# A linear recurrence in eight chunks: one copy changes engine, and the finishing of each chunk's outputs moves from a stage of its own into the next chunk

## The reference, cut to what matters

```python
def step(state, inp):                       # for each of 1024 tokens, per head
    r_t, w_t, k_t, v_t, kk_t, a_t = inp
    sa = jnp.einsum('bhvk,bhk->bhv', state, -kk_t)
    state = (state * w_t[:, :, None, :] + sa[..., None] * (kk_t * a_t)[:, :, None, :]
             + v_t[..., None] * k_t[:, :, None, :])
    return state, jnp.einsum('bhvk,bhk->bhv', state, r_t)
...
mu = jnp.mean(y, axis=-1, keepdims=True)    # group norm over the 64 values of a head
var = jnp.mean(jnp.square(y - mu), axis=-1, keepdims=True)
y = ((y - mu) * lax.rsqrt(var + RWKV_GN_EPS)).reshape(B, S, C)
y = y * lnx_g.astype(f32) + lnx_b.astype(f32)
bonus = jnp.sum((r_h * k_h * r_k).astype(f32), axis=-1, keepdims=True) * v_h.astype(f32)
y = (y + bonus.reshape(B, S, C)) * g.astype(f32)
```

## Time and profile before

| | us |
|---|---|
| three runs | 3178.64, 3179.79, 3193.91 |
| median | 3179.79 |
| profiled execution, its own time | 3191.28 |
| its span, first to last instruction | 3189.7 |
| `rwkv_chunks`, 601 to 973 | 372 |
| `rwkv_outputs`, 973 to 1018.8 | 46 |
| engines busy over the span | PE 2767.5, DVE 1088.9, ACT 632.5, POOL 514.5 |

### The profile page before, as it was taken

How to read it: one execution, slowest core, us unless ns; L and a number is a source line. 1 busy time by engine, 2 the same in 40 slices (tenths; PEclk the granted TensorE clock), 3 DMA queues, 4 the chain that set the end, 5 groups by cost and what they waited for, 6 DMA issues and landing times. The chain is left out here.

```text
span 3189.7 us, 52841 instructions
## 1 busy us (share of the span) xinstructions
PE 2767.5 (87%) x19900; PEld 2592.0 (81%) x19901; DVE 1088.9 (34%) x2428; ACT 632.5 (20%) x1210; POOL 514.5 (16%) x753
## 2 busy tenths in 40 slices
PE   8899897588883979893999999999999999999980
PEld 7876685377773968793999999999999999999980
DVE  2118322344545322434322222232232232322228
ACT  3119412112213122320111011111111111111111
POOL 0000001333330000015112121211212212112104
PEclk9999998799996989896999999999999999999995
DMA  7110111000002120216888778888888888887877
GB/s 236 31 33 1 40 46 28 9 17 18 18 11 73 40 73 14 62 41 197 292 287 292 256 262 281 288 295 287 295 282 293 294 287 282 294 283 262 283 240 270
DMA packets 340492, 549.48 MB, mean 172 GB/s; under 512 B 41120, under 2 KB 120864, under 8 KB 340384
## 3 DMA queue, kind: packets, MB, share of 16 engines
q1 hardware_dynamic: 321056, 505.56, 46.4%
q0 software_dynamic: 19360, 42.87, 4.6%
HBM read 507.06 MB, written 41.31 MB: 172 GB/s over the span
## 5 line engine op out<-in xcount | busy, mean ns | idle before, releaser
L2385 PE MATMUL experts_up<-experts_xs,g_pieces 128*128 128x144 f32 (+1 forms) x8192 | 1035.7, 289 | 66.6 <-issue 38.0
L2385 PEld LDWEIGHTS experts_up<-experts_xs,g_pieces 128*128 128x128 f32 x8192 | 1029.1, 197 | 73.7 <-issue 73.7
L2408 PE MATMUL experts_down<-experts_hs,g_across 128*128 128x144 f32 (+1 forms) x3072 | 394.6, 289 | 3.8 <-issue 3.3
L2408 PEld LDWEIGHTS experts_down<-experts_hs,g_across 128*128 128x128 f32 x3072 | 387.6, 190 | 7.7 <-issue 7.6
L2267 POOL DMA_INDIRECT experts_x<-h_rows,experts_index x198 | 191.7, 968 | 1146.9 <-DVE experts_xs L2314 1092.1
L2344 DVE TENSOR_SCALAR experts_glu<-experts_up,experts_bias 128x176 f32<-128x176 f32 x256 | 102.5, 400 | 712.5 <-PE experts_up L2385 712.5
L2294 ACT ACTIVATE experts_sig<-experts_glu 128x352 f32<-128x352 f32 x128 | 63.6, 497 | 963.4 <-DVE experts_lin L2346 963.4
L2301 ACT ACTIVATE experts_yT<-experts_down,experts_bias 128x176 f32<-128x176 f32 x256 | 99.7, 406 | 394.8 <-PE experts_down L2408 142.7
L2335 DVE COPY experts_bias<-g_bias 128x24 f32 x32 | 5.8, 180 | 400.8 <-ACT experts_yT L2301 400.8
L2397 PE MATMUL experts_down<-experts_hs,g_across 128*128 128x144 f32 (+1 forms) x1024 | 133.2, 288 | 0.0
L2397 PEld LDWEIGHTS experts_down<-experts_hs,g_across 128*128 128x128 f32 x1024 | 130.1, 190 | 0.0
(11 more groups left out here) (414 smaller groups left out, 4097.5 us busy)
## 6 DMA issues: line engine op xcount, KB each, us to landing
g_pieces<-in_w_dram SPq DMA_DIRECT2D x132, 2048.0 KB
g_across<-in_w_dram SPq DMA_DIRECT2D x64, 2048.0 KB, 9.3
y_rows<-experts_y SPq DMA_DIRECT2D x132, 192.0 KB, 3.8
g_across<-in_w_ckv_dram SPq DMA_DIRECT2D x8, 1024.0 KB, 10.2
rkv_raw<-in_w_in_dram SPq DMA_DIRECT2D x13, 512.0 KB, 3.9
diff_qk_raw<-in_w_in_dram SPq DMA_DIRECT2D x9, 512.0 KB, 4.0
cross_q_raw<-in_w_cq_dram SPq DMA_DIRECT2D x9, 512.0 KB, 3.7
m_u<-in_x_dram SPq DMA_DIRECT2D x8, 512.0 KB, 10.2
```

Source lines behind the costliest of these rows:

```text
L2385: ins = pe.matmul(up[:, u % 4, l * N:l * N + w], raw[c][:, k, at:at + 255:2], xs[:, k, 0:w], start=(k == 0), stop=(k == 7), skip_group_che ...
L2408: ins = pe.matmul(down[:, n % 4, 0:w], raw[4 + n // 4][:, k, (n % 4) * P:(n % 4 + 1) * P], hs[:, k, 0:w], start=(k == 0), stop=(k == 7), s ...
```

## The change

1. The copy to `vc` leaves GpSimd and becomes an ACT copy, `values(i + 1)`. It is made in chunk i behind the level-6 copies, once DVE's bonus product has read the old values.
2. `rwkv_outputs` is removed. For each chunk t its work is done inside chunk t + 1, 128 x 512 elements an instruction, and for the last chunk behind the loop. DVE gets `centred` (sum, mean, subtract) behind `state_in`, `deviation` behind its level-4 adds and the making of `ab`, `scaled` (reciprocal, rows) behind part 4 of `prepare`, and `gated` (bonus, gate) behind its level-6 adds. ACT gets `square` behind the three copies, `root` (Sqrt) behind the level-5 copies and `gain` (four Identity activations) ahead of its wait for the solution. TensorE gets `turn_rows`, four transposes into `mixed[:, 0]` between the p and the q products of level 6.
3. `rows` takes the place of `power[:, 1]`, squares go to `a` and the gained columns to `sig`, each in places of chunk t that nothing reads any more.
4. The first chunk is written out too, because it has no chunk before it: one chunk, a loop of six, one chunk.

```diff
-            with eng.Fori(0, NCH - 1) as i:
-                chunk(i, True)
-            chunk(NCH - 1, False)
+            chunk(0, True)
+            with eng.Fori(1, NCH - 1) as i:
+                chunk(i, True, i - 1)
+            chunk(NCH - 1, False, NCH - 2)
 # GpSimd
-                    pool.wait_ge(dve_steps.sem, dve_steps.value("bonus", i - 1))
-                    pool.wait_ge(pe_steps.sem, pe_steps.value("turn", i - 1))
-                    pool.wait_ge(pool_steps.sem, pool_steps.so_far(i))
-                    pool.tensor_copy(vc[:], u[:, 8:12, now]).then_inc(*pool_steps.step("v"))
 # ScalarE
+                def values(i):
+                    act.copy(vc[:], u[:, 8:12, ds(i * P, P)]).then_inc(*ahead_act.step("v"))
+                def square(t):
+                    act_out.round()
+                    act.wait_ge(dve_out.sem, dve_out.value("subtract", t))
+                    act.activation(a[:, :, ds(t * P, P)], outputs[:, :, ds(t * P, P)], ACT.Square).then_inc(*act_out.step("square"))
+                def root(t):
+                    act.wait_ge(dve_out.sem, dve_out.value("variance", t))
+                    act.activation(variance[:], variance[:], ACT.Sqrt).then_inc(*act_out.step("root"))
+                def gain(t):
+                    act.wait_ge(pe_out.sem, pe_out.value("turn", t))
+                    for c in range(CT):
+                        act.activation(sig[:, c, ds(t * P, P)], mixed[:, 0, c * P:(c + 1) * P], ACT.Identity,
+                                       bias=C.vector["lnx_b"][:, c:c + 1], scale=C.vector["lnx_g"][:, c:c + 1]).then_inc(*act_out.step(f"col{c}"))
...
                         if more and l == LEVELS[0]:
                             prepare(i + 1)
+                        if t is not None and l == LEVELS[1]:
+                            root(t)
+                    if more:
+                        act.wait_ge(dve_steps.sem, dve_steps.value("bonus", i))
+                        values(i + 1)
+                    if t is not None:
+                        gain(t)
                     act.wait_ge(pe_steps.sem, pe_steps.value("solve", i))
 # VectorE
+                def centred(t):
+                    y = grouped(outputs[:, :, ds(t * P, P)])
+                    dve_out.round()
+                    dve.wait_ge(act_steps.sem, act_steps.value("y", t))
...
+                    dve.tensor_reduce(mean[:].rearrange("p (c g) -> p c g", c=CT), y, AX, ALU.add).then_inc(*dve_out.step("sum"))
...
+                        if t is not None and l == LEVELS[0]:
+                            deviation(t)
                         if more and l == LEVELS[1]:
                             prepare(i + 1, 4)
+                        if t is not None and l == LEVELS[1]:
+                            if more:
+                                dve.wait_ge(ahead_dve.sem, ahead_dve.value("k", i + 1))
+                            scaled(t)
+                    if t is not None:
+                        gated(t)
                     dve.wait_ge(pe_steps.sem, pe_steps.value("state", i))
 # TensorE
+                def turn_rows(t):
+                    pe_out.round()
+                    pe.wait_ge(dve_out.sem, dve_out.value("rows", t))
+                    for c in range(CT):
+                        ins = pe.transpose(mixed[:, 0, c * P:(c + 1) * P], rows[:, c, :], C.ident[:])
+                    ins.then_inc(*pe_out.step("turn"))
...
-                    pe.wait_ge(pool_steps.sem, pool_steps.value("v", i))
+                    pe.wait_ge(ahead_act.sem, ahead_act.value("v", i))
...
+                        if n == 2 and t is not None:
+                            if more:
+                                pe.wait_ge(ahead_dve.sem, ahead_dve.value("ab0", i + 1))
+                            else:
+                                pe.wait_ge(act_steps.sem, act_steps.value("rhs", i))
+                            turn_rows(t)
                         for g in groups:
                             pe.wait_ge(act_steps.sem, act_steps.value(f"l{l}_p{g}", i))
...
+                    if t is not None:
+                        pe.wait_ge(act_out.sem, act_out.value(f"col{CT - 1}", t))
                     for c in range(CT):
                         pe.matmul(mixed[:, 0, c * P:(c + 1) * P], ar[:, c, 1, :], state[:, c, :], start=(c == 0),
```

More of the change, by code:

```diff
@@ L928, with rwkv_chunks @@
 KAPPA = float(np.exp(-0.5))
-def rwkv_chunks(nc, u, a, sig, kkn, fall, masks, outputs, C):
+def rwkv_chunks(nc, u, a, sig, kkn, fall, masks, outputs, gate, C):
     corr_mask, level_mask, blocks, own = masks
@@ L970, in rwkv_chunks @@
         state = S.sb("state", [P, CT, P])
+        rows = power[:, 1]
+        mean, variance = S.sb("mean", [P, H]), S.sb("variance", [P, H])
         pairs = S.ps("pairs", [P, 2, 512])
@@ L981, in rwkv_chunks @@
                             [f"l{l}_p{g}" for l in LEVELS for g in groups] + ["solve", "y"])
-        pool_steps = S.steps("pool", ["v"] + [f"part{l}" for l in LEVELS])
+        pool_steps = S.steps("pool", [f"part{l}" for l in LEVELS])
         dve_steps = S.steps("vector", ["r", "edge", "state_in"] + [f"mask{h}" for h in range(H)] + ["inv", "invT", "bonus"] +
@@ L993, in rwkv_chunks @@
         lower_out, block_in, solved_out, compact_in = (S.sem(n) for n in ("lower_out", "block_in", "solved_out", "compact_in"))
+        act_out = S.steps("act_out", ["square", "root"] + [f"col{c}" for c in range(CT)])
+        dve_out = S.steps("vector_out", ["sum", "mean", "subtract", "squares", "variance", "rstd", "rows", "bonus", "gate"])
+        pe_out = S.steps("products_out", ["turn"])
         wiped = S.sem("wiped")
@@ L1121, in chunk @@
                              mixed[:, 0, :].rearrange("p (c n) -> p c n", n=P)).then_inc(*act_steps.step("y"))
+                for s in (act_out,):
+                    act.sem_inc(s.sem, s.start)
                 prepare(0)
+                values(0)
                 all_chunks(act, chunk)
+                square(NCH - 1)
+                root(NCH - 1)
+                gain(NCH - 1)
+                act.wait_ge(act_out.sem, act_out.end(NCH))
                 act.wait_ge(act_steps.sem, act_steps.end(NCH))
@@ new lines, in deviation, with scaled @@
+                def deviation(t):
+                    dve.wait_ge(act_out.sem, act_out.value("square", t))
+                    dve.tensor_reduce(variance[:].rearrange("p (c g) -> p c g", c=CT), grouped(a[:, :, ds(t * P, P)]), AX,
+                                      ALU.add).then_inc(*dve_out.step("squares"))
+                    follows(t)
+                    dve.tensor_scalar(variance[:], variance[:], 1.0 / 64, 64e-5, ALU.mult, ALU.add).then_inc(*dve_out.step("variance"))
+                def scaled(t):
+                    dve.wait_ge(act_out.sem, act_out.value("root", t))
+                    dve.reciprocal(mean[:], variance[:]).then_inc(*dve_out.step("rstd"))
+                    follows(t)
+                    dve.tensor_tensor(grouped(rows), grouped(outputs[:, :, ds(t * P, P)]), spread(mean[:]),
+                                      ALU.mult).then_inc(*dve_out.step("rows"))
@@ L1164, in chunk, with gated @@
+                def gated(t):
+                    cols, now = sig[:, :, ds(t * P, P)], ds(t * P, P)
+                    dve.wait_ge(act_out.sem, act_out.value(f"col{CT - 1}", t))
+                    dve.tensor_tensor(cols, cols, u[:, 0:4, now], ALU.add).then_inc(*dve_out.step("bonus"))
+                    follows(t)
+                    dve.tensor_tensor(gate[:, :, now], cols, gate[:, :, now], ALU.mult).then_inc(*dve_out.step("gate"))
+                def chunk(i, more, t=None):
                     now = ds(i * P, P)
@@ L1227, in _ @@
                     prepare(0, part_of)
+                dve.sem_inc(dve_out.sem, dve_out.start)
                 all_chunks(dve, chunk)
+                for step in (centred, deviation, scaled, gated):
+                    step(NCH - 1)
+                dve.wait_ge(dve_out.sem, dve_out.end(NCH))
                 dve.wait_ge(dve_steps.sem, dve_steps.end(NCH))
@@ L1337, in _ @@
                 products_ab(0)
+                pe.sem_inc(pe_out.sem, pe_out.start)
                 all_chunks(pe, chunk)
[L1341 to L1364, removed]
[L1365 to L1421 removed]
```

85 lines of the change are left out of this document (22 added, 63 removed).

## The result

The changed kernel takes 3135.4 us (median of 4 runs, 3128.9 to 3143.2), the kernel before 3180.3 us (median of 4). The ratio is 0.9851, with a 95% interval of 0.9815 to 0.9886: 45 us less, where 71 were forecast. The point 3109 was missed by 26 us, and the median lies 2 us above 3133, the upper end of the range and the time that rival A had been given; counted by the ratio from the 3179.8 on which the forecast stood, it is 3132.4, just inside. The range reached that far only because rival A was taken into it.

A forecast was written before the change was run, and what follows sets the result against it. Bound: stages in series, TensorE waiting for the values' copy each chunk, nearly idle in the outputs stage. Gains of 33.9 us to the last y copy and 36.8 behind it, 70.7 off 3179.8, gave 3109 us; range 3093 to 3121, to 3133 with rival A.

The forecast's parts named there:

- rival A: TensorE's clock falls in every chunk, as the rows wait leaves it idle 1.9 us: 24 us, 3133 us; chance 0.13.
- The wait for the values: Chunk start: TensorE no longer waits for GpSimd's copy, saving 5.4 us a chunk plus 1.9 of half clock behind it.
- Chunk 0: First chunk: masks and right side come earlier, 6.5 us gained less 2.5 for half clock; gain 4.0 us.
- The tail: From the last y copy to the outputs' end: 9.7 us instead of 46.5, gain 36.8 us.
- centred: DVE work at a chunk's start makes the first mask late: cost 0.3 us a chunk, bounds 0 and 0.6.
- deviation: DVE work between `ab` and the level-5 adds makes the third add late: cost 0.1 us a chunk.
- rows wait: Level 6: TensorE waits for the rows and transposes them before the q products; cost 2.6 us a chunk, bounds 2.0 to 3.4.
- Chunk 7: Last chunk, without preparation, so rows are ready earlier and TensorE waits about 0.7 us: period 36.1 us instead of 42.4.
- The table loads: Two ScalarE loads a chunk of 1.28 us for Sqrt beside Exp, hidden in ScalarE's waits: cost 0.
- The clock: TensorE's granted clock in the changed chunks stays near 1.00, so the chunk periods carry no cost for half clock.
- signs of being wrong: Transposes at a chunk's start still waiting, a period above 43 us, or a stage clock under 0.9.
- rival C: The relay (`ab` to `compact`) is slowed by added DVE work and becomes the bound: 9 us, 3118 us; chance 0.07.

The follow-up runs named there:

- e1: Kernel before with only the copy to `vc` moved to ScalarE behind the level-6 copies, `rwkv_outputs` kept: 3134.2 us, ratio 0.9849.
- e3: Changed kernel with 14 transposes of the identity added ahead of the wait for the rows in level 6, filling TensorE's pause: 3160.3 us, ratio 0.9920.
- e7: Changed kernel with Square in place of Sqrt in `root`, so no activation table is loaded inside the chunks: 3162.8 us, ratio 0.9935.
- e11: Changed kernel with 28 transposes of the identity written out behind the last chunk, none in the chunks: 3171.5 us on a slower chip, ratio 0.9917.
- e10: e4 with only the subtract of `centred` moved behind the second mask: 3118.2 us on a slower chip, ratio 0.9763.
- e4: Changed kernel with the rows' transposes behind the solution products, `scaled` behind the level-6 adds, `gain` behind the solution's copy: 3118.2 us, ratio 0.9804.
- e8: e1 with a DVE reduce of 1536 elements added behind `state_in`, lengthening TensorE's pause at the masks: 3134.1 us, ratio 0.9846.
- e9: e1 with a DVE reduce of 896 elements behind part 4 of `prepare`, awaited by TensorE ahead of level 6's q products: 3172.1 us, ratio 0.9967.
- e6: Changed kernel with rows moved as in e4, `centred` moved ahead of the level-4 adds and `square` behind the Exps: 3118.0 us, ratio 0.9797.

## Why the prediction was right or wrong

- **The wait for the values (gain 5.4 + 1.9 us a chunk): right.** The transposes start ahead of the y copy, and e1 alone gave periods of 37.2 us; 36.9 was worked out.
- **Chunk 0 (gain 4.0): 5.3.** From the stage's start to the first y copy it took 65.5 us and takes 60.2.
- **The tail (gain 36.8): 37.2.** From the last y copy to the first load behind the stage it was 48.1 us and is 10.9.
- **centred (0.3), deviation (0.1), rows wait (2.6): right in sum.** The first mask came at 703.28 + 3.67, 0.4 us later than 3.29 allowed. The rows wait is 1.71 us of pause and 0.5 of transposes, 2.2. Periods at full clock were 39.4 and 39.5 (e3, e7, e11), and 40.2 for chunk 1 in the kernel after; 39.9 was the sum. In chunk 1 DVE waited 1.5 us for the relay, where the forecast had 1 us and called it covered.
- **Chunk 7 (36.1): 37.4,** with 3.4 us of it at half clock.
- **The table loads (0): right.** Their place was not as told: the first stands ahead of the copy of v and makes it 0.5 us late, which nobody waits for.
- **The clock (0): wrong, and with it the sum.** The seven periods took 299.7 us, 24.2 more than the 275.5 forecast, and five of them hold 10 to 14 us at half clock. Two of the forecast's own signs of being wrong came true: periods above 43 us, and a clock in the stage under 0.9 (0.87). This is rival A, priced at 24 us and given 0.13. The step that failed is the argument against it: that 1.56 us of idle time had left the clock at 1.00. It was one case, read as a threshold, against a pause of which the forecast itself said 1.9 us; and the rows of before had a fall without a long pause, which should have counted for more. Rival A also looked at the rows wait alone. Two of the five stretches began behind the mask pause, which grew from 0.64 us to between 1.1 and 1.3 because of `centred` and which the forecast counted only as 0.3 us of lateness. That A's 24 us met the measured 24.2 is luck: there were five long stretches and not seven falls, and one cost not 3.4 but 4 to 5.6 us, since the stretches are of 10 to 14 us and not of 7.
- **The range.** The bounds as listed add up to 13.5 us below and 13 above the point, 3095.5 to 3122, not 3093 to 3121. Nothing hangs on it, since the range was drawn up to A.
- **The relay (rival C):** not the bound in the kernel after, but the next one. In e1 DVE waits for `compact` 10.1 us in seven chunks, in e10 14.7.

What stays open: which pauses of this length bring the clock down. It fell in three periods of e4 behind pauses of 0.93 to 1.19 us and in none of e8 behind 1.28 us, and it fell behind three of six rows pauses in the kernel after and behind one of six in e11, whose chunks are the same. e10 and e4 differ in the mask pause, but e10 also moved the periods a little, and one execution of each was looked at.

## What to carry to other kernels

Work that is hidden beside TensorE's still costs where TensorE has to wait for it in the middle of a dense stretch: 2.1 us of pause cost 4.6 to 6.3 us a chunk here, because the clock fell behind it (e9). Put the product that needs the hidden work where its input has long been ready, into a PSUM bank that is free there, rather than where the bank happens to be free: that was worth 17 us of the stage (370.8 to 353.9), and with the second new pause taken away as well 31 (339.7), with the same work. Filling only one of two pauses with work that nobody needs gave nothing that could be seen. And when two parts of a change are meant to add up, run each alone: one moved copy held nearly the whole gain.

## What the runs showed of the hardware

- A half-clock stretch (1.2 GHz) came while TensorE was over 90% busy, right behind one pause: 9.49 busy of 10.0 us at 0.50 (e9). It did not come behind pauses of 1.28 us in e8, came behind each pause of 2.1 us in e9, and in e4 came behind three of seven pauses of 0.93 to 1.32 us.
- Code that is added can cost some 21 us far behind the edit: 28 more transposes in it (two TensorE instructions each), in the chunks or behind them, took the instruction queue from 54 to 75 or 76 packets and put three or four waits of 6.6 to 8.0 us into the experts' loop.
- A DVE operation that reads two SBUF tiles and started 0.3 us behind a GpSimd operation took 2.42 us instead of 0.69 and ended 0.56 us behind GpSimd's; so it was three times in e6. The mask products of 0.55 us, which read PSUM, ran beside the same GpSimd operation without delay.
